# One layer's projection stage and chunk scan: the next block's norm inside the block, later loads of the turned tokens, and S5 table work spread over later scan passes

## The reference, cut to what matters

```python
hn = rmsnorm(h, mix_norm[l])
a_q, a_f, a_i, a_g, b_y, b_x, c_u, d_z = jnp.split(hn @ w_in[l], IN_SPLITS, axis=-1)
# HGRN2: log_f = logaddexp(log(lb), log1p(-lb) + log_sigmoid(f)); cum = cumsum(log_f) in a chunk
#        gate: o * norm_g * silu(g_in)
# RG-LRU: a = exp(log_a); u = sqrt(-expm1(2 log_a)) * (gate_i * xc); h = scan(a, u); out = h * gelu(y)
# RWKV-7: decay, a, kk, k, bonus, g from mixed tokens
# S5:     a_bar = exp(lam * dt); powers of a_bar; b_bar = (a_bar - 1) / lam * b
```

## Time and profile before

| | |
|---|---|
| runs | 3288.15, 3288.4, 3290.76 us, median 3288.4 |
| profiled execution | 3286.77 us, span 3284.6 us |
| PE busy | 3087.9 us (94% of the span) |
| PEld, DVE, ACT, POOL busy | 77%, 66%, 41%, 15% |
| mean granted PE clock | 0.974 of 2.4 GHz |
| projection stage | 0 to 598 us, PE busy 556.4 us |
| chunk scan and the way into it | 598 to 1002 us, PE busy 351.1 us |
| chain that ended last | PE, lines 2921 and 2936 (the MLP's matmuls) 39%, nothing of the projection named |

### The profile page before, as it was taken

One profiled execution on the slowest core, in us unless ns is written; L12 is line 12 of the kernel. 1 busy time (PEld: TensorE's weight loads), 2 busy tenths in 40 slices (PEclk: granted clock), 3 DMA queues, 4 the chain that ended last, 5 costly groups with the idle time before them and its releaser, 6 DMA issues. The chain is left out here.

```text
span 3284.6 us, 51424 instructions
## 1 busy us (share of the span) xinstructions
PE 3087.9 (94%) x20672; PEld 2521.7 (77%) x20672; DVE 2161.8 (66%) x3314; ACT 1337.5 (41%) x2133; POOL 493.7 (15%) x650
## 2 busy tenths in 40 slices
PE   8999999699998889999999989999899999999998
PEld 6777776588887668767888768888688887788887
DVE  6666574677756557644544577667866776787886
ACT  5646555455552322112333343333433333444443
POOL 4333333467750001100000000000000000000000
PEclk9999999799999999999999989999899999999999
DMA  6363645222210164330111323323322234777774
GB/s 215 93 212 93 215 139 175 97 68 74 67 51 8 66 231 165 122 122 28 63 64 64 115 97 115 108 104 128 122 105 108 103 115 133 256 210 229 246 219 125
DMA packets 200073, 416.21 MB, mean 127 GB/s; under 512 B 15280, under 2 KB 99504, under 8 KB 193456
## 3 DMA queue, kind: packets, MB, share of 16 engines
q1 hardware_dynamic: 199856, 413.18, 38.2%
HBM read 295.66 MB, written 117.46 MB: 126 GB/s over the span
## 5 line engine op out<-in xcount | busy, mean ns | idle before, releaser
L2921 PE MATMUL ffn_ps<-ffn_t_p,ffn_w_p 128*128 128x512 f32 x2640 | 619.8, 394 | 2.6 <-DVE ffn_w_p L3094 2.6
L2921 PEld LDWEIGHTS ffn_ps<-ffn_t_p,ffn_w_p 128*128 128x128 f32 x2640 | 496.6, 188 | 118.8 <-DVE ffn_w_p L3094 3.6
L2936 PE MATMUL ffn_ps<-ffn_t_p_parts 128*128 128x512 f32 x1416 | 329.5, 392 | 7.2 <-DVE ffn_t_p_parts L3236 7.2
L2936 PEld LDWEIGHTS ffn_ps<-ffn_t_p_parts 128*128 128x128 f32 x1416 | 267.3, 189 | 64.7 <-DVE ffn_t_p_parts L3236 8.0
L485 PE MATMUL proj<-hn_high,w_high 128*128 128x512 f32 x672 | 278.7, 421 | 17.7 <-ACT t_ag L554 14.6
L485 PE MATMUL proj<-hn_low,w_high 128*128 128x512 f32 x672 | 267.3, 402 | 5.9 <-DVE hn_low L693 4.6
L397 POOL TENSOR_TENSOR w_low<-w_ring,w_high 128x1024 fp32r<-128x1024 f32 x84 | 211.5, 2521 | 370.1 <-ACT w_high L530 370.1
L485 PE MATMUL proj<-hn_high,w_low 128*128 128x512 f32 x672 | 260.5, 395 | 0.0
L2947 ACT ACTIVATE ffn_w_p<-ffn_w_p_sums 128x512 fp32r<-128x512 f32 x132 | 83.5, 633 | 343.0 <-DVE ffn_w_p_sums L3115 342.8
L485 PEld LDWEIGHTS proj<-hn_high,w_high 128*128 128x128 f32 x672 | 128.3, 191 | 55.0 <-ACT t_ag L554 16.3
L485 PEld LDWEIGHTS proj<-hn_low,w_high 128*128 128x128 f32 x672 | 129.0, 192 | 46.0 <-DVE hn_low L693 13.8
(11 more groups left out here) (496 smaller groups left out, 6481.4 us busy)
## 6 DMA issues: line engine op xcount, KB each, us to landing
ffn_ring<-in_w_up SPq DMA_DIRECT2D x44, 1024.0 KB, 5.4
ffn_ring<-in_w_down SPq DMA_DIRECT2D x88, 512.0 KB, 5.4
w_ring<-in_w_feat SPq DMA_DIRECT2D x84, 512.0 KB, 3.7
ffn_ring<-scratch_values SPq DMA_DIRECT2D x88, 257.0 KB, 4.6
scratch_gates<-ffn_gate SPq DMA_DIRECT2D x44, 512.0 KB, 2.6
ffn_ring<-scratch_gates SPq DMA_DIRECT2D x88, 256.0 KB, 3.8
scan_in<-scratch_scan SPq DMA_DIRECT2D x16, 896.0 KB, 4.6
scratch_values<-ffn_raw SPq DMA_DIRECT2D x22, 513.0 KB, 3.6
```

The lines of the kernel that those rows point to most:

```text
L2921: mm = pe.matmul(bank(name, s), w_part(name, a)[:, k * P:(k + 1) * P], t_part(name, b)[:, k * TB:(k + 1) * TB], start=k == a == b == 0, st ...
L2936: mm = pe.matmul(ps[:, DOWN_BANKS[2 * t + c]], down_part(n, x)[:, HID + t * TC:HID + (t + 1) * TC], down_part(n, y)[:, c * DH:(c + 1) * DH ...
```

## The change

In the projection, in every block:

- the norm of the next block's tokens moves forward. `squares` come after tiles 1, 3, 5 and 8 (before: 2, 5, after `k_sq`, after `gi`), x loads in steps 3, 5, 7, 9, `norm_root` behind the Sqrt of `inv`, `mean_square` behind the chunk sums of the decay, `diagonals` behind the RWKV-7 vectors, `spread_rstd` after tile 15, `normed` behind `bonus`;
- x_t is loaded in steps 12 to 15;
- the clamped f and its logarithm live in `T["inv"]`. So tiles 15 and 16 are copied to `T["ag"]` early, as plain copies behind the Exp of `e` and behind the logarithm of lb, each with its `high_behind`; one Silu over both follows the Tanh, then tile 17 is taken, then the roots of `om`. The wait for `lf_done` goes;
- on DVE the chunk sum `cum` and the gate factor come behind `low_tokens`; SP's stores of the last block are ordered for it.

In the scan: S5's decay and angle move into pass -1's first slot, the sines to ACT's end of pass -1, the memsets to pass 0's first slot and the first powers to its second, powers 1 to 3 and 4, 5 to pass 1, powers 6, 7 and the gain to pass 2, all that follows two passes on. The memsets ahead of `kr` now hold `scores_d[0]` and the buffers of u = 0 only; the rest follow `kr`, and `scores_d[1]` is cleared in pass -1's second slot.

The diff, without the lines that only declare signals (lines are moved left by eight columns):

```diff
@@ -327,10 +327,10 @@
         features("scan", "k", T["k"])
-        sp.wait_ge(*om_ready.at(p))
-        features("scan", "cum", T["cum"])
         sp.wait_ge(*vaux_out.at(p, 1))
         tokens("vd", v_tok[:])
+        sp.wait_ge(*cum_ready.at(p))
+        features("scan", "cum", T["cum"])
         sp.wait_ge(*ag_ready.at(p))
@@ -363,13 +363,13 @@
                 load_x(p + 1, 0)
-            if has_next and n in (7, 10, 13):
-                j = (7, 10, 13).index(n)
+            if has_next and n in (5, 7, 9):
+                j = (5, 7, 9).index(n)
                 sp.wait_ge(*sumsq.at(p + 1, j))
                 load_x(p + 1, j + 1)
-            if has_next and 8 <= n < 12:
+            if has_next and 12 <= n < 16:
                 sp.wait_ge(*hn_ready.at(p))
-                load_x_turned(p + 1, range((n - 8) * KT // 4, (n - 7) * KT // 4))
+                load_x_turned(p + 1, range((n - 12) * KT // 4, (n - 11) * KT // 4))
             if n == 9:
@@ -488,7 +488,7 @@
             small_products(n)
-            if n == 18 and has_next:
+            if n == 15 and has_next:
                 spread_rstd(p + 1)
@@ -552,8 +552,7 @@
             own.done(act.activation(dst, proj[:, n % 3], func), proj_out, n)
-            if n not in (15, 16):
-                high_behind(n)
+            high_behind(n)
@@ -567,8 +566,8 @@
             take(n, z[:, n, 1:])
-            if has_next and n in (2, 5):
-                squares(p + 1, (2, 5).index(n))
+            if has_next and n in (1, 3, 5):
+                squares(p + 1, (1, 3, 5).index(n))
             if n == 3:
@@ -582,24 +581,24 @@
         take(8, bx[:, 1, LRU_TAPS - 1:])
+        if has_next:
+            squares(p + 1, 3)
         act.wait_ge(*stored.at(p, back=1))
...
             own.done(act.activation(T["sq"][:, t], z[:, 1 + t, 1:], ACT.Square, scale=col("rw_k_k", t)), k_sq, t)
-        if has_next:
-            squares(p + 1, 2)
         for t in range(G2):
...
         own.done(act.activation(T["inv"][:], T["inv"][:], ACT.Sqrt), ss_root)
+        if has_next:
+            norm_root(p + 1)
         for name, bias, m0 in (("gr", "lru_ba", 6), ("gi", "lru_bx", 8)):
...
             take(11 + (m0 - 6) // 2, T["f"][:, (m0 - 6) // 2])
-        if has_next:
-            squares(p + 1, 3)
         for t in range(G2):
@@ -610,30 +609,26 @@
         own.done(act.activation(T["e"][:], T["e"][:], ACT.Exp, scale=-1.0))
-        high_behind(15)
+        take(15, T["ag"][:, 0])
         act.wait_ge(*f_clamped.at(p))
-        own.done(act.activation(T["ag"][:], T["ag"][:], ACT.Exp, scale=-1.0))
+        own.done(act.activation(T["inv"][:], T["inv"][:], ACT.Exp, scale=-1.0))
...
         for t in range(G2):
-            last = act.activation(T["ag"][:, t], T["ag"][:, t], ACT.Ln, bias=1.0, scale=C["lb"][:, t:t + 1])
+            last = act.activation(T["inv"][:, t], T["inv"][:, t], ACT.Ln, bias=1.0, scale=C["lb"][:, t:t + 1])
         own.done(last, lb_log)
-        high_behind(16)
+        take(16, T["ag"][:, 1])
         for t in range(G2):
...
                      th_ready, t)
-        act.wait_ge(*lf_done.at(p))
-        for t in range(G2):
-            take(15 + t, T["ag"][:, t], ACT.Silu)
-        if has_next:
-            norm_root(p + 1)
+        own.done(act.activation(T["ag"][:], T["ag"][:], ACT.Silu), ag_gated)
+        take(TOK, late_tile(0))
         for t in range(G2):
...
             own.done(act.activation(T["gr"][:, t], T["gr"][:, t], ACT.Sqrt), om_root, t)
-        take(TOK, late_tile(0))
         for m in range(2 * G2):
@@ -731,6 +726,8 @@
                      csig_done, t)
+        if has_next:
+            mean_square(p + 1)
         for t in range(G2):
@@ -746,26 +743,33 @@
                                               ALU.mult, ALU.mult), rk_ready, t)
+        if has_next:
+            diagonals(p + 1)
         for t in range(G2):
             dve.wait_ge(*proj_out.at(p, 11 + t))
-            own.done(dve.tensor_scalar(T["ag"][:, t], T["f"][:, t], -40.0, None, ALU.max),
+            own.done(dve.tensor_scalar(T["inv"][:, t], T["f"][:, t], -40.0, None, ALU.max),
                      *((f_clamped,) if t else ()))
...
             own.done(dve.tensor_tensor(T["bonus"][:, t], z[:, 5 + t, 1:], aux_v[:], ALU.mult), vaux_out, 4 + t)
+        if has_next:
+            normed(p + 1)
         dve.wait_ge(*f_log.at(p))
...
         for t in range(G2):
-            own.done(dve.tensor_tensor(T["e"][:, t], T["e"][:, t], T["ag"][:, t], ALU.add),
-                     *((lf_done,) if t else ()))
-        if has_next:
-            mean_square(p + 1)
-        for t in range(G2):
-            own.done(dve.tensor_tensor_scan(T["cum"][:, t], chunk_start, T["e"][:, t], 0.0, ALU.mult, ALU.add))
-        if has_next:
-            diagonals(p + 1)
+            own.done(dve.tensor_tensor(T["e"][:, t], T["e"][:, t], T["inv"][:, t], ALU.add))
+        def sum_logs():
+            for t in range(G2):
+                own.done(dve.tensor_tensor_scan(T["cum"][:, t], chunk_start, T["e"][:, t], 0.0, ALU.mult, ALU.add),
+                         *((cum_ready,) if t else ()))
+
+        def norm_gate():
+            for t in range(G2):
+                dve.wait_ge(*ag_gated.at(p))
+                own.done(dve.tensor_scalar(T["ag"][:, t], T["ag"][:, t], col("hg_norm", t), None, ALU.mult),
+                         *((ag_ready,) if t else ()))
@@ -773,8 +777,6 @@
             own.done(dve.tensor_tensor(T["xc"][:, t], T["xc"][:, t], T["gi"][:, t], ALU.mult))
-        if has_next:
-            normed(p + 1)
         for t in range(G2):
@@ -783,12 +785,10 @@
                      *((out_b,) if t else ()))
-        for t in range(G2):
-            dve.wait_ge(*proj_out.at(p, 15 + t))
-            own.done(dve.tensor_scalar(T["ag"][:, t], T["ag"][:, t], col("hg_norm", t), None, ALU.mult),
-                     *((ag_ready,) if t else ()))
         if has_next:
             low_tokens(p + 1)
+        sum_logs()
+        norm_gate()
         dve.wait_ge(*vaux_done.at(p, 6))
@@ -851,13 +851,17 @@
-def s5_first_powers(dve, me, S5, sines):
-    v, re, im, L = S5["v"], S5["re"], S5["im"], S5_BLOCK
-    ts, tt = dve.tensor_scalar, dve.tensor_tensor
-    for x in (S5["b_pad"][:], S5["c_pad"][:, :, 0:L - 1], re[:, 0], im[:, 0]):
+def s5_zeros(dve, me, S5):
+    re, im = S5["re"], S5["im"]
+    for x in (S5["b_pad"][:], S5["c_pad"][:, :, 0:S5_BLOCK - 1], re[:, 0], im[:, 0]):
 last = dve.memset(x, 0.0)
...
     me.done(dve.memset(re[:, 0], 1.0))
+
+
+def s5_first_powers(dve, me, S5, sines):
+    v, re, im = S5["v"], S5["re"], S5["im"]
+    ts, tt = dve.tensor_scalar, dve.tensor_tensor
     dve.wait_ge(*sines.at(0))
@@ -1189,21 +1193,25 @@
                            ps_g[0:HD, :, P:2 * P].rearrange("p g (t n) -> p g t n", t=G2), ACT.Copy, scale=-1.0).then_inc(cx_out.sem, 1)
-
-    me, v = Own(act, own["s5_act"]), S5["v"]
+        if i < 0:
+            s5_sines()
+
+    def s5_sines():
+        act.wait_ge(*decay_arg.at(0))
+        me.done(act.activation(s5_v[1][:], s5_v[1][:], ACT.Exp))
+        act.wait_ge(*angle.at(0))
+        me.done(act.activation(s5_v[3][:], s5_v[2][:], ACT.Sin))
+        me.done(act.activation(s5_v[4][:], s5_v[2][:], ACT.Sin, scale=0.5), sines)
+
+    me, s5_v = Own(act, own["s5_act"]), S5["v"]
     act.wait_ge(*loaded[0].at(0))
...
     act.wait_ge(*s5_loaded.at(0, 1))
-    me.done(act.activation(v[0][:], S5["raw"][:, 2], ACT.Exp), dt_done)
+    me.done(act.activation(s5_v[0][:], S5["raw"][:, 2], ACT.Exp), dt_done)
     exp_halves(0, 0, 0)
...
     prepare_a(0, 0)
-    act.wait_ge(*decay_arg.at(0))
-    me.done(act.activation(v[1][:], v[1][:], ACT.Exp))
-    act.wait_ge(*angle.at(0))
-    me.done(act.activation(v[3][:], v[2][:], ACT.Sin))
-    me.done(act.activation(v[4][:], v[2][:], ACT.Sin, scale=0.5), sines)
     iterations(run)
@@ -1311,16 +1319,21 @@
         if i < 0:
-            s5_first_powers(dve, s5, S5, sines)
-        if i < 1:
-            for power in (1, 2, 3) if i < 0 else (6, 7):
+            s5_decay_and_angle(dve, s5, S5, s5_loaded, dt_done, decay_arg, angle)
+        elif i == 0:
+            s5_zeros(dve, s5, S5)
+        elif i == 1:
+            for power in (1, 2, 3):
                 s5_power(dve, s5, S5, power)
-        elif i == 1:
+        elif i == 2:
+            for power in (6, 7):
+                s5_power(dve, s5, S5, power)
+        elif i == 3:
             dve.wait_ge(*s5_tables.at(0))
...
             s5_input(dve, s5, S5, 0)
-        elif i < 2 + S5_BLOCK + 1:
-            s5_output_row(dve, s5, S5, i - 2)
+        elif i < 4 + S5_BLOCK + 1:
+            s5_output_row(dve, s5, S5, i - 4)
         if has_a:
@@ -1330,14 +1343,18 @@
         if i < 0:
+            start.done(dve.memset(scores_d[1][:], 0.0))
+        elif i == 0:
+            s5_first_powers(dve, s5, S5, sines)
+        elif i == 1:
             for power in (4, 5):
                 s5_power(dve, s5, S5, power)
-        elif i == 0:
+        elif i == 2:
```

(22 more changed lines are left out.)

## The result

| | before | after |
|---|---|---|
| runs, median (lowest to highest) | 3289.58 us (3288.15 to 3290.99, 4 runs) | 3263.1 us (3262.12 to 3263.91, 4 runs) |
| ratio to before, 95% interval | | 0.9911 [0.9899, 0.9923] |
| span of the profiled execution | 3284.6 | 3260.3 |
| mean granted PE clock | 0.974 | 0.976 |
| end of the projection's last small product | 598.0 | 577.2 |

Faster by 26.5 us; forecast was 3261.7. The projection gave 20.8 (forecast 20.7), the scan 6.6 (forecast 6). That is 27.4 together, and the spans differ by 24.3: what lies behind the scan, which the change leaves alone, took 3.1 longer in this execution. The sum is right. Whether each edit is worth what its term says is another matter, and most of what follows is about it.

The account below looks back on a forecast made before the run. PE, busy 94% of the span, was taken as the bound, gains being its idle or slow time. Terms -16.2 - 1.5 - 6 + 3 - 6 = -26.7 from 3286.77 give 3260.1, as run median 3261.7; range 3252 to 3271.

Parts of the forecast that it names:

- Part 3: Tile 10's late weights: PE's need comes earlier than the stores shift, so waits and slow time grow, +3 us.
- Part 2: Block end: `low_tokens` begins 0.8 and ends 8.2 after tile 0 began; -2 us at each of three boundaries, -6.
- Part 1: Tiles 15 and 16 copied early: the stall before tile 18 and slow pace behind it go, -16.2 us; last block -1.5.
- The time cannot all be kept: Last block: PE waits again for RG-LRU's squares, which hang on ACT and DVE, so only -1.5 us.
- 3.5 a block: Stored sums and gate norm behind `low_tokens` are covered by tile 0 and small products; without that cover, 3.5 us a block.
- The same bytes: Late-weight stretch: half of x_t (1.0 MB) leaves, x tiles 2 and 3 (1.0 MB) enter; moved x_t counted at nothing.
- Part 4: Scan's start: S5's slot in pass -1 shrinks, and with it PE's wait and slow matmuls, -6 us.
- the 5.2: Scan pass -1: gain from DVE's S5 slot going from 7.9 us to 2.7.
- the second one: Rival: weights become the bound, PE time saved before tile 8 is waited back, Parts 2 and 3 +6 to +9; 3276, chance 0.17.
- the third rival: The stall only moves: PE waits 3 to 4 us after tile 18 instead; Part 1 -4, 3274 or 3284; chance 0.06.
- 0.2 us of margin: After tile 18: tile 17's take ends at 282.7, PE comes at 282.9; nothing counted, 0.5 us allowed.
- its turned tokens: Slower rival: late turned tokens hold DVE at `normed`, delaying `om`, h scan and `low_tokens`; at 12 us a block 3298, chance 0.04.

Follow-up runs that it names:

- E1: The changed kernel with tiles 15 and 16 again taken late, as two Silu takes after the Tanh: 3263.38 us, ratio 0.9913.
- E8: The changed kernel with ACT copying the weights of the next block's tile 2 only after the last token tile: 3268.85 us, ratio 0.9922.
- E9: The changed kernel with the next block's `normed` again behind the products that make `om`: 3270.11 us, ratio 0.9932.
- E10: E7 with `normed` also put back behind the products that make `om`: 3275.61 us, ratio 0.9949.
- E7: The changed kernel with the undoings of E1 and E3 together: 3264.6 us, ratio 0.9908.
- E5: The changed kernel itself, run once more as yardstick: 3262.93 us, ratio 0.9904.
- E2: The changed projection with the chunk scan and S5 tables of the kernel before: 3269.59 us, ratio 0.9936.
- E4: The changed kernel with the turned tokens loaded in steps 8 to 11 again: 3276.4 us, ratio 0.9955.
- E11: The changed kernel with the takes of small products 2 and 3 ahead of tile 10's weight copy on ACT: 3259.06 us, ratio 0.9895.
- E12: E11 plus RG-LRU's last-block sum of squares moved into tile 20 and the S5 gain halved over passes 2 and 3: 3244.95 us, ratio 0.9855.
- E3: The changed kernel with `cum` and the gate norm ahead of `low_tokens` again: 3275.51 us, ratio 0.9952.

## Why the prediction was right, and where not

**By place.** The forecast says where PE's time goes: by its terms the four stretches should lose 5.4, 6.4, 6.4 and 2.5 us, and they lost 6.0, 7.0, 6.3 and 1.4. So it was close in every stretch, and that is not luck; that the whole comes within 0.1 is, since the loss of 3 in Part 3 was not found and Part 2 and the last block gave less than booked. What the terms do not give is what each edit is worth, and my expectation for E1 used them so.

**Part 1, the stall (-16.2 and -1.5).** The mechanism was right: the wait of 3.65 is gone in all four blocks. The step that failed is "I count it for blocks 0, 1, 2", taken as the worth of the early takes. E1 puts 12.0 of the 14.6 us of stall back and costs about 2 us, since tile 0 then passes 3.2 faster. In the middle blocks the early takes give 1.4 to 3 us each (138.5 and 138.6 in E1; 137.1 and 137.2, and 135.5 and 136.8, in two executions of the changed kernel). In the last block they seem to cost 1.3 to 2.4 (180.3 in E1; 181.6 and 182.7), which is within the noise: PE comes 3.65 earlier to the sum of squares, waits 4.6 in place of nothing, and goes slow behind it. "The time cannot all be kept" was right; that the block gains 1.5 was not.

**Part 2, the block's end (-6).** Start and end of `low_tokens` were met within 0.4 us, and the three hold-ups by POOL too. (The start before was taken from the earlier trace rows as 2.55 behind tile 0 in every block; in the first one it was 4.9.) PE passes tile 0 in 8.8 to 9.1 us, where it took 10.4 to 10.6, so some 1.5 each of the 2 forecast. The Trainium skill (SBUF — State Buffer, "Who interferes with whom") says that a DVE instruction with two SBUF inputs and a GpSimd instruction that reads SBUF exclude each other. The runs agree: 7.11 with POOL's product inside, 4.9 without (E8, E9). `cum` and the gate norm ahead of `low_tokens` cost 9 to 11 us, as the "3.5 a block" said. What has no price in the prediction is the place of `normed`: behind `om` it costs 3 to 5 (E9) or 9 (E10).

So 20.7 forecast and 20.8 measured is a right sum over places with a wrong account of causes: the whole gain was booked on the edit at the place where PE's wait was seen. From before to E10 (586.0 to 573.1) the norm's other pieces, the gone wait for `lf_done` and the later x_t give 13 us together, more than half, for edits to which the prediction gave nothing of their own; `normed` gives 9 more (E7); the takes and the stored pieces on top of it nothing more. By the starts of tile 0, 7.3 of the 13 are in the last block, where the wait of 2.24 for `t_sq` is gone and PE's last eleven microseconds ran at a clock of 1.00 in place of 0.84. Which of the edits gives how much of the 13 was not tried.

**Part 3, late weights (+3).** This term is not borne out. The waits at line 426 went from 3.5 to 5.7 in the profiled execution, but came to 3.2 in E5 and 2.4 in E2, the same projection; the hold on ACT for tile 10 was 5.3 to 8.7 in the changed kernel and E5, and 5.6 to 8.1 before. So 20.7 fits 20.8 with a loss of 3 in it that the runs do not show. Two things were wrong in it besides. "The same bytes" made x_t's move nothing, and loading it early costs 6 to 8 us in the new order (E4). And I took the late weights for PE's bound, where it was the queue behind them on ACT (E11).

**Part 4, the scan (-6).** 6.6 on the two profiled executions, 5.1 on the means, 6 to 7 where the pace behind the gain's wait is the same. Pass -1 gave more than the 5.2, the rest as forecast; the gain's wait was found where it was expected and taken out in E12.

**The rivals.** The sum of the second one does not come out as written: with +6 to +9 for Parts 2 and 3 its other terms give 3271 to 3274, not 3276. The stall did move in a sense, as the third rival says, but to `hn_low` and `t_sq`, not to tile 17, where the 0.2 us of margin held but for 0.58 in the last block. Weights as the bound was not this kernel, but it is 6.6 us of issue time away (E8). `normed` never waited for its turned tokens.

## What to carry to other kernels

A wait seen at one place is not the worth of the edit that takes it away: that pays only what the next place does not ask back (4.6 us gained at tile 18, 3.2 asked back at tile 0). Before adding up such terms, follow the other engines to where the busiest one meets them next and subtract, and look for idle time there into which moved work falls. Test parts in pairs: E1 and E3 alone gave 2 and 10 us, together 0, and neither alone would have told that. When an engine holds for a late transfer, look at what stands behind the held instruction in its queue before treating the transfer itself.

## What the runs showed of the hardware that was not expected

A wait's price is not its length, and not fixed by it either. In E4 two waits of 3.39 and 3.38 us at the same line, one block apart, left the granted clock at 1.00 and brought ten microseconds to 0.66; the waits of 4.6 and 1.1 in the last block went together with 8.3 (E12). Behind the gain's wait of 3.1 in the scan the next ten microseconds were granted 0.75 to 0.83 in six executions and 0.50 in seven, E5 and the changed kernel, one program, on different sides; with it the scan differs by 4 to 6 us. The scan, the same instructions, took 385.1 to 391.6 us in ten executions; differences of kernels by ratio hold that much of it. POOL's product holds a one-input DVE instruction too: in E8 the two gate factors took 3.11 us beside one, and 1.01 in the kernel after:

```profile
298.06 2.40 POOL L397 TENSOR_TENSOR w_low<-w_ring,w_high 128x1024 fp32r<-128x1024 f32 x1 [10.58 <-ACT w_high L530]
...
297.64 3.11 DVE L773 TENSOR_SCALAR t_ag<-t_ag,prm_sb 128x512 f32<-128x512 f32 x2
```
